# The last two expert pairs' rows go to their tokens by a matrix product, the other pairs' rows are loaded and added earlier

## The reference

```
h2 = x1 * (1 + scale2) + shift2                      # (512, 1024)
group = top-1 of softmax(h2 @ w_rg + b_rg)           # 4 groups
e1, e2 = top-2 of softmax(expert logits in the group)# 8 experts a group
w1, w2 = p1/(p1+p2) * g_prob, p2/(p1+p2) * g_prob
moe = sum over the two experts of  w * (silu(h2 @ w_gate[e]) * (h2 @ w_up[e])) @ w_down[e]
out = layer_norm(ALPHA * x1 + gate2 * moe) * ln2_g + ln2_b
```

## Time and profile before

| | |
|---|---|
| median of three runs | 629.87 us |
| profiled execution | 629.51 us |
| its span, first to last instruction | 627.7 us |
| PE busy | 514.9 us (82%) |
| VectorE busy | 282.1 us (45%) |
| GpSimd busy | 128.2 us (20%) |
| ScalarE busy | 100.1 us (16%) |
| memory read and written | 159.6 and 12.6 MB, 274 GB/s over the span |
| mean granted clock of PE | 0.921 |

### The profile page before, as it was taken

The page is one execution under the profiler, slowest core; times in us unless marked ns, Lnnn a source line. Parts: engine busy times, 40 slices in busy tenths (PEclk is TensorE's granted clock), DMA queues, the critical chain, the costliest instruction groups (busy, mean ns, idle before and its releaser), DMA issues.

```text
span 627.7 us, 6651 instructions
## 1 busy us (share of the span) xinstructions
PE 514.9 (82%) x2521; PEld 287.7 (46%) x2521; DVE 282.1 (45%) x490; ACT 100.1 (16%) x161; POOL 128.2 (20%) x117
## 2 busy tenths in 40 slices
PE   0999999999999998999981599999987788887200
PEld 0994445864454443444561355555543444444000
DVE  2557465564748293355537622232322211221295
ACT  0110010132314131201130112111111101111010
POOL 2000000014406040225454211112111111000066
PEclk9987999999999999899975699999998988899755
DMA  8991667774124063497065299999999999997343
GB/s 290 302 311 47 202 201 238 245 236 148 65 73 133 3 239 135 180 416 302 34 234 200 81 394 414 414 416 417 417 417 417 418 417 417 416 419 320 131 164 134
DMA packets 67011, 164.10 MB, mean 261 GB/s; under 512 B 7560, under 2 KB 44460, under 8 KB 58796
## 3 DMA queue, kind: packets, MB, share of 16 engines
q1 hardware_dynamic: 58416, 149.96, 62.6%
q0 software_dynamic: 4608, 8.40, 3.7%
q10 hardware_dynamic: 3964, 5.44, 2.5%
HBM read 159.58 MB, written 12.58 MB: 274 GB/s over the span
## 4 chain that ended last, share of the span: by engine, by line
PE 62%; DMA 16%; DVE 10%; SPq 6%; POOL 3%; issue 2%; ACT 1%; POOLq 1%; DVEq 0%
DMA w_gu<-in_w_up_dram 12%; PE ps L1237 12%; PE ps L1127 10%; PE ps L1090 9%; PE ps L1172 9%; PE ps L1246 5%; PE ps L1097 4%; SPq L320 4%; PE ps L1048 3%; DMA stage<-in_w_ada_dram 2%; DVE acc_rows L715 2%; SPq L324 2%; PE ps L1230 2%; PE ps L1116 1%; PE ps L1162 1%
## 5 line engine op out<-in xcount | busy, mean ns | idle before, releaser
L1237 PE MATMUL ps<-w_gu,xT 128*64 128x256 f32 x1024 | 126.2, 402 | 24.9 <-DMA w_gu<-in_w_up_dram 21.8
L1237 PEld LDWEIGHTS ps<-w_gu,xT 128*64 128x64 f32 x1024 | 75.5, 145 | 66.2 <-DMA w_gu<-in_w_up_dram 17.3
L1127 PE MATMUL ps<-hT,stage 128*128 128x512 f32 x192 | 84.8, 595 | 0.0
L972 DVE TENSOR_TENSOR ysb<-ps,rows_gate 64x512 f32<-64x512 f32 x64 | 44.1, 689 | 52.5 <-PE ps L1246 52.1
L964 DVE TENSOR_TENSOR hid<-ps,silu_sb 128x128 f32<-128x128 f32 x32 | 9.3, 292 | 123.6 <-ACT silu_sb L642 109.7
L1246 PE MATMUL ps<-w_dn,hidT 128*64 128x512 f32 x256 | 61.3, 599 | 0.5 <-ACT hidT L636 0.4
L1090 PE MATMUL ps<-hT,stage 128*128 128x512 f32 x128 | 57.4, 612 | 1.1 <-DVE hT L731 1.1
L465 POOL DMA_INDIRECT y_dram<-ysb,slot_row x16 | 16.1, 1008 | 202.0 <-DVE ysb L972 202.0
L715 DVE SCALAR_TENSOR_TENSOR acc_rows<-stage,csil,acc_rows 128x256 f32<-128x256 f32 x112 | 55.3, 493 | 4.0
L1172 PE MATMUL ps<-wo,mixT 128*128 128x512 f32 x128 | 55.4, 592 | 0.0
L1127 PEld LDWEIGHTS ps<-hT,stage 128*128 128x128 f32 x192 | 35.5, 190 | 41.0 <-issue 41.0
(11 more groups left out here) (184 smaller groups left out, 505.7 us busy)
## 6 DMA issues: line engine op xcount, KB each, us to landing
w_gu<-in_w_gate_dram SPq DMA_DIRECT2D x32, 1024.0 KB, 20.6
w_gu<-in_w_up_dram SPq DMA_DIRECT2D x32, 1024.0 KB, 23.0
w_dn<-in_w_down_dram SPq DMA_DIRECT2D x32, 1024.0 KB, 24.1
stage<-in_w_ada_dram SPq DMA_DIRECT2D x24, 1024.0 KB, 7.9
stage<-in_w_in_dram SPq DMA_DIRECT2D x12, 1024.0 KB, 10.0
wo<-in_w_out_dram SPq DMA_DIRECT2D x1, 4096.0 KB, 14.9
y_tok<-y_dram SPq DMA_DIRECT2D x8, 512.0 KB, 7.5
xs<-in_x_dram ACTq DMA_DIRECT2D x1, 2048.0 KB, 14.1
```

The source lines that it names most:

```text
L972: ins = w.tensor_tensor(ysb[u][e * HD:(e + 1) * HD, b * 512:(b + 1) * 512], ps[b * HD:(b + 1) * HD, 6 + e, :], gate2r[b * HD:(b + 1) * HD, ...
L1127: ins = t.matmul(ps[:, 6], st[:, k, (f % 2) * P:(f % 2 + 1) * P], hT[:, k], start=k == 0, stop=k == KC - 1)
L1237: ins = t.matmul(ps[a * SLOTS:(a + 1) * SLOTS, 2 + e, 0:2 * P], xT[u][:, k, e * SLOTS:(e + 1) * SLOTS], w_gu[slot][e][:, :, k, a * P:(a + ...
```

## The change

1. Pairs 14 and 15 (NTURN = 2) are no longer scattered. Their rows stay in `ysb`; for each VectorE builds a matrix `turn_to` (128 slots by 512 tokens) that holds a slot's weight in its token's column, and PE multiplies it with `ysb` and sums over both pairs (`rows_to_tokens`). VectorE adds the product from PSUM to each tile.
2. A slot's weight comes from a small DRAM tensor: SyncE stores the tokens' weights, GpSimd gathers them for the two pairs' slots.
3. The rows of `y_dram` that belong to those pairs' slots are set to zero by two scatters from a zeroed `ysb` buffer before the first pair.
4. The `y_tok` loads are issued when pair 13 has been scattered, ahead of the loads of g2r and bb2r, and VectorE's adds are placed among its steps for pair 15.
5. The branch for overflow blocks moves on all engines from the end to between pairs 12 and 13, with semaphores of its own; the loop now ends before pair 12, which with pairs 13, 14 and 15 stands written out. The gather for pair 15 moves behind that branch.

Where a line holds only dots, lines are left out; on SyncE and PE the branch for overflow blocks stands at the dots ahead of the last pairs.

```diff
--- before.py
+++ after.py
+CUT = NPAIR - 3
+NTURN = 2
...
+        turn_to = [at(f"turn_to{n}", [P, T], PAIR1 + (32 + 2 * n) * KB) for n in range(NTURN)]
+        iota_t = at("iota_t", [P, T], PAIR1 + 36 * KB)
```

SyncE:

```diff
+            sp.wait_ge(wk_ready, 1)
+            sp.dma_start(w_dram.rearrange("(i p k) o -> p i (k o)", p=P, k=2), wk_rows[:]).then_inc(st_wk, 16)
...
+            refill(NPAIR // RING, 0)
+            sp.wait_ge(dn_done, NE - 2 * RING)
+            load_dn(0, 1, NPAIR - 1 + HALF)
+            sp.wait_ge(dn_done, 2 * (CUT + 1))
             for u in range(RING):
-                sp.wait_ge(scattered[u], 16 * (NPAIR // RING + (u == 0)))
+                sp.wait_ge(scattered[u], 16 * len(range(u, NPAIR - NTURN, RING)))
             for i in range(TC):
                 for k in range(2):
                     sp.dma_start(y_tok[i][:, k], ...).then_inc(ld_y[i][k], 16)
+            sp.wait_ge(dn_done, NE - 3)
+            sp.dma_start(g2r[:], ln2_g[0].partition_broadcast(P)).then_inc(ld_g2, 16)
+            sp.dma_start(bb2r[:], ln2_b[0].partition_broadcast(P)).then_inc(ld_g2, 16)
```

GpSimd:

```diff
+            g.memset(ysb[0][:], 0.0).then_inc(zero_ready, 1)
+            pool.wait_ge(zero_ready, 1)
+            for n in range(NTURN):
+                scatter(NPAIR - NTURN + n, ysb[0], zeroed)
...
+                if j == CUT - 1:
+                    beyond_slots()
+                    pool.wait_ge(xe_done, CUT)
+                    gather(CUT + 2, xg[0], gathered[0])
+                    g.memset(w_slot[:], 0.0).then_inc(w_slot_clear, 1)
+                    pool.wait_ge(w_slot_clear, 1)
+                    pool.wait_ge(st_wk, 16)
+                    for n in range(NTURN):
+                        slot_weight(n)
+            pool.wait_ge(gu_done, 2 * (CUT + 1))
+            g.iota(iota_t[:], [[1, T]], base=0, ...).then_inc(iota_t_ready, 1)
```

VectorE:

```diff
+            def add_rows(i, k):
+                dve.wait_ge(x1_done, i + 1)
+                dve.wait_ge(ld_y[i][k], 16)
+                link(w.scalar_tensor_tensor(out=xs[:, i], in0=y_tok[i][:, k], scalar=wk[:, k, i:i + 1],
+                                            in1=xs[:, i], op0=ALU.mult, op1=ALU.add))
+
+            def slots_to_tokens():
+                dve.wait_ge(w_slot_got, 16 * NTURN)
+                dve.wait_ge(iota_t_ready, 1)
+                link(w.tensor_copy(tok_f[:], slot_tok[:, NPAIR - NTURN:NPAIR]))
+                for n in range(NTURN):
+                    w.tensor_scalar(turn_to[n][:], iota_t[:], tok_f[:, n:n + 1], w_slot[:, n:n + 1],
+                                    ALU.is_equal, ALU.mult).then_inc(turn_to_ready, 1)
+
+            i = CUT // RING
+            pair(i, 1, fresh=True)
+            pair(i, 2)
+            slots_to_tokens()
+            add_rows(0, 0)
+            add_rows(0, 1)
+            hidden(NE - 2, 0)
+            y_out(NE - 3, 1, 2)
+            add_rows(1, 0)
+            add_rows(1, 1)
+            add_rows(2, 0)
+            hidden(NE - 1, 1)
+            y_out(NE - 2, 0, 0, i + 1)
+            add_rows(2, 1)
+            y_out(NE - 1, 1, 0)
+            add_rows(3, 0)
+            add_rows(3, 1)
 
             dve.wait_ge(ld_g2, 32)
             for i in range(TC):
-                dve.wait_ge(x1_done, i + 1)
-                for k in range(2):
-                    dve.wait_ge(ld_y[i][k], 16)
-                    link(w.scalar_tensor_tensor(out=xs[:, i], in0=y_tok[i][:, k], scalar=wk[:, k, i:i + 1],
-                                                in1=xs[:, i], op0=ALU.mult, op1=ALU.add))
+                dve.wait_ge(turned, i + 1)
+                link(w.tensor_tensor(xs[:, i], xs[:, i], ps[:, 2 * i:2 * i + 2].rearrange("p b n -> p (b n)"), ALU.add))
                 for n in range(2):
                     did(w.bn_stats(bn[:, n], xs[:, i, n * 512:(n + 1) * 512]))
```

PE:

```diff
+            pair(CUT // RING, 0)
+            turn(2 * CUT - 1, 1)
+            finish(2 * CUT - 1, 1, 0, CUT // RING)
...
+            pair(CUT // RING, 1, fresh=True)
+            pair(CUT // RING, 2)
             pair(NPAIR // RING, 0, last=True)
             turn(NE - 1, 1)
             finish(NE - 1, 1, 0, NPAIR // RING)
+            def rows_to_tokens(i):
+                for n in range(NTURN):
+                    pe.wait_ge(turn_to_ready, n + 1)
+                    pe.wait_ge(y_ev, 2 * (NPAIR - NTURN + n) + 2)
+                    for b in range(2):
+                        ins = t.matmul(ps[:, 2 * i + b], turn_to[n][:, i * P:(i + 1) * P],
+                                       ysb[(NPAIR - NTURN + n) % RING][:, b * 512:(b + 1) * 512],
+                                       start=n == 0, stop=n == NTURN - 1, skip_group_check=True)
+                ins.then_inc(turned, 1)
+            for i in range(TC):
+                rows_to_tokens(i)
```

More of the change, by code:

```diff
@@ L52 @@
 RING = 3
-LAST0 = (NPAIR + RING - 1) // RING
+CUT = NPAIR - 3
+NTURN = 2
+BEFORE_CUT = CUT // RING + 1
 SKIP = 4096
@@ L368, in _ @@
             with sp.If(more > 0):
-                with sp.Fori(0, NOVP) as j:
-                    sp.wait_ge(dn_done, NE + 2 * j)
+                sp.wait_ge(dn_done, 2 * CUT)
+                for j in range(NOVP):
+                    if j > 0:
+                        sp.wait_ge(ov_dn, 2 * j)
                     for e in range(2):
-                        ex = sp.value_load(blk_exp[0:1, bass.ds(j + e * NOVP, 1)], min_val=0, max_val=NE - 1)
+                        ex = sp.value_load(blk_exp[0:1, j + e * NOVP:j + e * NOVP + 1], min_val=0, max_val=NE - 1)
                         for g, w in enumerate((w_gate, w_up)):
@@ L497, in _ @@
                 scatter(j, ysb[u], scattered[u])
[L499 to L507, removed]
+                if j == CUT - 1:
+                    beyond_slots()
+                    pool.wait_ge(xe_done, CUT)
+                    gather(CUT + 2, xg[0], gathered[0])
[5 more added lines that the diff above has]
+            pool.wait_ge(gu_done, 2 * (CUT + 1))
+            g.iota(iota_t[:], [[1, T]], base=0, channel_multiplier=0, allow_small_or_imprecise_dtypes=True
+                   ).then_inc(iota_t_ready, 1)
             def scale_shift(i):
@@ L656, in _ @@
                 pair(0, u, first=u == 0)
-            with act.Fori(1, NPAIR // RING) as i:
+            with act.Fori(1, CUT // RING) as i:
                 for u in range(RING):
                     pair(i, u)
-            pair(NPAIR // RING, 0, last=True)
-            hid_t(NE - 1, 1)
+            pair(CUT // RING, 0)
+            hid_t(2 * CUT - 1, 1)
             act.wait_ge(flag_ready, 1)
@@ L968, in y_out @@
                 dve.wait_ge(dn_done, y + 1)
+                if isinstance(y, int) and y == 0:
+                    dve.wait_ge(zeroed, 16 * NTURN)
                 if e == 0 and (not isinstance(i, int) or i > 0):
@@ L975, in y_out, with pair @@
                 ins.then_inc(y_ev, 1)
-            def pair(i, u, first=False):
+            def pair(i, u, first=False, fresh=False):
                 j = RING * i + u
@@ L981, in pair @@
                     overflow_slots()
-                else:
+                elif not fresh:
                     y_out(2 * j - 1, 1, (u - 1) % RING)
@@ L1262, in finish, with pair @@
                 down(e, u, dn_done)
-            def pair(i, u, first=False, last=False):
+            def pair(i, u, first=False, last=False, fresh=False):
                 j = RING * i + u
                 pu, pi = ((u - 1) % RING, i - 1 if u == 0 else i)
-                if not first:
+                if not first and not fresh:
                     turn(2 * j - 1, 1)
@@ L1294, in _ @@
                 pair(0, u, first=u == 0)
-            with pe.Fori(1, NPAIR // RING) as i:
+            with pe.Fori(1, CUT // RING) as i:
                 for u in range(RING):
                     pair(i, u)
+            pair(CUT // RING, 0)
+            turn(2 * CUT - 1, 1)
+            finish(2 * CUT - 1, 1, 0, CUT // RING)
+            pe.wait_ge(flag_ready, 1)
+            more = pe.value_load(flag[0:1, 0:1], min_val=0, max_val=NOVB)
+            with pe.If(more > 0):
+                pe.wait_ge(y_ev, 2 * CUT)
+                pe.wait_ge(xe_ev, CUT + 1)
+                with pe.Fori(0, NOVP) as j:
+                    pe.wait_ge(ov_gathered, 16 * (j + 1))
+                    expert_rows(0, ov_xe)
+                    pe.wait_ge(ov_xe_ev, j + 1)
+                    pe.wait_ge(ov_ld, 96 * (j + 1))
+                    for e in range(2):
+                        gate_up(e, 0, 0, ov_gu)
+                        pe.wait_ge(ov_hid, 2 * j + e + 1)
+                        t.transpose(ps[:, 4 + e, 0:P], hid[e][:], ident[:]).then_inc(ov_tr, 1)
+                        pe.wait_ge(ov_tr_ev, 2 * j + e + 1)
+                        down(e, 0, ov_dn)
+                    pe.wait_ge(ov_y, 2 * j + 2)
+            pair(CUT // RING, 1, fresh=True)
+            pair(CUT // RING, 2)
             pair(NPAIR // RING, 0, last=True)
```

91 lines of the change are left out of this document (52 added, 39 removed).

## The result

The changed kernel takes 632.8 us at the median of 18 runs (631.07 to 635.81), the kernel before 629.88 on the same chips (18 runs, 627.46 to 632.76): a ratio of 1.0054 (95% interval 1.0035 to 1.0073), slower. The forecast was 633.5.

What follows compares the result with a forecast made beforehand. The weight stream sets the pace, then a chain with nothing beside it, then GpSimd. 4.8 us late less 1.2 gives 3.6: span 627.7 becomes 631.3, plus 1.8 and 0.4 makes 633.5; range 627 to 638.

Steps and rivals of the forecast that it cites:

- x: Reference point in each trace for the kernel's end: the issue of the last two loads of w_dn.
- The mechanism: Kernel's end: y_tok loads land behind the weights, VectorE waits, hidden(30) comes 12 us later, first inverse deviation 4.8 us later.
- The loads' price: End of SP's queue: slowest engine takes 2.0 us per MB; weights done at 582.1, first y_tok 583.0, eighth 590.
- GpSimd's chain: From the first inverse deviation on: four tiles' chain carried over, 1.2 us back from idling; step changes within 2 us.
- The added transfers: Between 346 and 358 us: zero scatters, a memset and the weights' store cost nothing; 2.4 us if in the stream.
- The waits: Near the end: VectorE waits from about 570 to 583.0 for y_tok; PE idles 11 us before its last gate-and-up block.
- low-clock rival: Products at the end run at half clock, 6.9 us a tile: 636.2; chance 0.12.
- partial: Slow DMA engine lags less: y_tok loads at 578 and 579, hidden(30) at 581, total 628.5; chance 0.08.
- early case: y_tok loads don't wait for the weights in their queue and land from about 574: 621.7; chance 0.12.

Runs made afterwards that it cites:

- order runs: Changed kernel with VectorE's y_tok adds moved later: after the last experts' steps 1.0114, two tiles' adds ahead of the first product add 0.9973, all ahead 0.9981.
- queue runs: Changed kernel with g2r and bb2r issued ahead of the y_tok loads, 1.0070; or with the y_tok loads issued from ScalarE's queue, 1.0023.
- other-queue run: Changed kernel with the eight y_tok loads issued from ScalarE's queue, not SyncE's: 631.52 us, 1.0023.

## Why the prediction was right, point by point

Taken from x, the forecast against the changed kernel (x = 556.05 for the forecast, 561.51 for the trace):

| step | forecast | measured |
|---|---|---|
| y_tok loads issued | x + 13.7 | 15.6 |
| first add starts | 27.0 | 27.7 |
| hidden(30) done | 30.0 | 30.7 |
| last gate-and-up block takes | 5.67 us | 5.68 us |
| last down product ends | 40.5 | 41.1 |
| first inverse deviation | 48.0 | 48.5 |
| span ends | 75.3 | 72.5 |

- *The mechanism holds in every link*: loads behind the weights, VectorE at add_rows(0, 0), PE's idle (12.29 us, forecast 11), a block that starts at half clock (granted 0.50 from 592 to 594 us), 10 us lost. The order runs and the queue runs move it as the theory says, and taking both waits away turns 1.0054 into 0.9973.
- *The loads' price* was 0.7 us short, and its rate rested on a misreading of the earlier trace rows. The 24.1 us there do not belong to the w_dn load of 556.05: the view of that one alone has no landing, and one appears when the second load, of 557.9, is taken in.

```profile
L324 SPq DMA_DIRECT2D w_dn<-in_w_down_dram x1: 1831/1831/1831, 556.1 to 556.1; - x1
...
L324 SPq DMA_DIRECT2D w_dn<-in_w_down_dram x2: 1831/2138/2446, 556.1 to 557.9; - x2
...
DMA to landing us min/median/max: 24.1/24.1/24.1
```

So the last weights were in at 582.0, and my 582.1 came from a wrong start and met it by luck. My rate of 2.0 us per MB, from 580.1 to 585.0, has no ground: from 582.0 to 585.0 there were 3.0 us for 1 MB and some part of a scatter. In the changed kernel the last weights landed at x + 26.3 (563.5 and 24.3 us) and the first y_tok load 1.4 us behind them; the last of the eight landed at 582.4 + 15.5 = 597.9, seven loads behind the first at 589.2, so about 1.2 us for half a MB, where I had put 1.0. The run with g2r in front moved the loads by 2.5 us for 1 MB.
- *GpSimd's chain was mis-sized*: I carried it over less 1.2 us, since VectorE would need less time for a tile. That part held: the second deviation starts 2.9 us behind the first, not 4.3. But the whole chain got 4.6 us shorter. The other 3.2 us are GpSimd's own steps (two inverse deviations at 0.55 and not 1.53, a shift at 0.19 and not 0.88, a scaling at 2.34 and not 3.15), since the y_tok adds no longer stand beside them. I had bounded this at 2 us either way, from GpSimd's full-tile steps, and not looked at its shortest ones: an inverse deviation of one column that takes 1.53 us was itself the sign.
- *The added transfers were not free*: the step "nothing: DMA is 0.26 busy" failed. The price was not in the megabytes but in the small pieces of one store, beside the gather that everything waits for.
- *The errors cancel*: from x on I had 2.8 us too much, at the start 2.9 too little, and the stretch between came out 1.0 shorter, which together is the 0.7 us between forecast and median within rounding. The waits, the largest part of the sum, were right by their own steps, the rest by luck.
- *The loads went out 1.9 us later* than forecast, since pair 13's scatter did (568.25): PE was late, having waited for the down weights of y = 25 and passed the branch. That scatter goes out at x + 6.7, without the branch at x + 5.9, before at x + 5.1. I had priced the down product of y = 25 at 2.5 us and left out the wait for its weights. It cost nothing, since the place in the queue set when the loads landed: without the branch they went out at x + 13.9, and the first add still came at x + 27.6.
- *The low-clock rival* didn't come: the product ran at full clock, 14.10 us for 32 instructions. The partial and the early case neither; the other-queue run gives 2.4 us at the span's end for 3.9 at the first load.

## What to carry to other kernels

A load moved forward in program order isn't moved forward in time when it stands behind a full queue: find what is issued ahead of it, on the slowest engine, before placing anything behind its wait. In a written-out engine program put what another engine's critical work needs first and optional work behind it, and do this for every wait, since taking out one only uncovers the next. VectorE's work on two operands in SBUF slows a chain that runs on GpSimd, but moving it ahead of the chain pays only if the chain starts later by less than it gets shorter: with all adds ahead that was 5.0 us later for 4.3 shorter. Where a profile names no releaser for an idle time, compare its end with the landing of what the next instruction reads.

## What the hardware showed that I had not expected

- 512 pieces of 8 bytes, 4 KB in all, cost some 2 us of a saturated stream (one slice of 5 us at 254 GB/s among 400 to 427), and 2.1 us of a gather issued at the same moment.
- PE idled 2.6 to 4.4 us for nothing that the profile names, and the idle ended in twelve profiles out of twelve within 0.2 us of the landing of the weights that it needed next.
- A one-column GpSimd operation took 0.55 or 1.53 us by what VectorE did beside it.
